# The modulation of the second block: from TensorE to ScalarE and GpSimd, and two half buffers beside the recurrence

## What is computed

```python
c_act = jax.nn.silu(c)                       # 1 x 1024
for l in range(2):
    mod = c_act @ w_ada[l] + b_ada[l]        # w_ada[l]: 1024 x 6144, mod: 1 x 6144
    sh_m, sc_m, gt_m, sh_f, sc_f, gt_f = jnp.split(mod, 6, axis=-1)
    h = rms_norm(x, g_mix[l]) * (1.0 + sc_m[:, None]) + sh_m[:, None]
    ...

def rwkv7_branch(u, ...):                    # first block
    for d, reverse in enumerate((False, True)):
        ...
        wkv = wkv + wkv7_scan(rh, heads(decay), kd, vh, -kk, kk * ah, reverse)
```

## Time and profile before

| | |
|---|---|
| median of the runs | 3211.61 us |
| profiled execution | 3216.43 us |
| its span | 3214.3 us, mean granted TensorE clock 0.940 |
| busy: TensorE | 2807.8 us (87%) |
| busy: VectorE | 1462.0 us (45%) |
| busy: ScalarE | 877.2 us (27%) |
| busy: GpSimd | 120.4 us (4%) |
| recurrence stage | about 122 to 790 us |

### The profile page before, as it was taken

How to read it: one execution, slowest core, us unless ns; L and a number is a source line. 1 busy time by engine, 2 the same in 40 slices (tenths; PEclk the granted TensorE clock), 3 DMA queues, 4 the chain that set the end, 5 groups by cost and what they waited for, 6 DMA issues and landing times.

```text
span 3214.3 us, 48264 instructions
## 1 busy us (share of the span) xinstructions
PE 2807.8 (87%) x21116; PEld 2057.9 (64%) x21116; DVE 1462.0 (45%) x2707; ACT 877.2 (27%) x1416; POOL 120.4 (4%) x199
## 2 busy tenths in 40 slices
PE   6898989868896877875798899999998888999999
PEld 5686767646573332321676667888876666778887
DVE  5545444467453110102565646434455665554433
ACT  3312212132430000001233353322223334433221
POOL 0010101010000000000000000000000000000000
PEclk9999999978997998997899999999999999999999
DMA  4353534332128999997233332333332342323332
GB/s 145 115 173 100 166 100 149 97 124 107 47 91 354 428 427 428 427 428 289 68 86 102 70 118 86 92 98 94 97 84 82 91 87 86 105 80 97 99 98 79
DMA packets 151816, 489.57 MB, mean 152 GB/s; under 512 B 13232, under 2 KB 41488, under 8 KB 139184
## 3 DMA queue, kind: packets, MB, share of 16 engines
q1 hardware_dynamic: 112256, 362.37, 31.5%
q0 software_dynamic: 26384, 97.32, 9.2%
q10 hardware_dynamic: 12960, 26.74, 2.6%
HBM read 456.49 MB, written 29.90 MB: 151 GB/s over the span
## 4 chain that ended last, share of the span: by engine, by line
PE 67%; DVE 14%; DMA 12%; ACT 5%; issue 2%; SPq 0%; POOL 0%; DVEq 0%; ACTq 0%; POOLq 0%
PE psum L154 64%; DMA wslot<-in_w_up 4%; DMA wslot<-in_w_gate 3%; DMA wslot<-in_w_down 3%; PE psum L157 3%; DVE halfL L163 2%; DVE sc__235 L193 1%; ACT halfH L160 1%; DVE m L190 1%; DVE slot L163 1%; DVE a20S L178 1%; DVE a21S L178 1%; ACT a1S L160 1%; DVE US L163 1%; DMA ada<-in_w_ada 0%
## 5 line engine op out<-in xcount | busy, mean ns | idle before, releaser
L163 DVE TENSOR_TENSOR halfL<-ring,halfH 128x1024 fp32r<-128x1024 f32 x302 | 367.5, 1221 | 684.6 <-ACT halfH L160 684.5
L160 ACT ACTIVATE halfH<-ring 128x1024 fp32r<-128x1024 f32 x302 | 316.5, 1053 | 808.4 <-PE psum L154 808.2
L154 PE MATMUL psum<-hH,halfH 128*128 128x512 f32 x1200 | 486.3, 405 | 9.7 <-DVE halfL L163 9.6
L154 PE MATMUL psum<-hL,halfH 128*128 128x512 f32 x1200 | 473.4, 394 | 0.0
L154 PE MATMUL psum<-hH,halfL 128*128 128x512 f32 x1200 | 472.3, 394 | 0.0
L154 PE MATMUL psum<-wslot,XT 128*64 128x512 f32 x1024 | 258.8, 664 | 73.7 <-DMA wslot<-in_w_gate 42.7
L154 PEld LDWEIGHTS psum<-hH,halfH 128*128 128x128 f32 x1200 | 228.5, 190 | 83.9 <-issue 23.4
L154 PEld LDWEIGHTS psum<-hH,halfL 128*128 128x128 f32 x1200 | 228.5, 190 | 49.6
L154 PEld LDWEIGHTS psum<-hL,halfH 128*128 128x128 f32 x1200 | 229.1, 191 | 44.6
L154 PEld LDWEIGHTS psum<-wslot,XT 128*64 128x64 f32 x1024 | 90.3, 152 | 241.3 <-issue 235.5
L154 PE MATMUL psum<-halfH,hH 128*128 128x512 f32 (+2 forms) x576 | 219.8, 382 | 11.8 <-DVE halfL L163 8.4
(11 more groups left out here) (446 smaller groups left out, 3909.9 us busy)
## 6 DMA issues: line engine op xcount, KB each, us to landing
wslot<-in_w_gate SPq DMA_DIRECT2D x32, 2048.0 KB, 30.0
...
ring<-in_w_in SPq DMA_DIRECT2D x120, 512.0 KB, 3.8
ada<-in_w_ada POOLq DMA_DIRECT2D x96, 512.0 KB, 4.2
ring<-in_w_gu SPq DMA_DIRECT2D x88, 512.0 KB, 3.6
ring<-in_w_down SPq DMA_DIRECT2D x44, 512.0 KB, 3.8
...
```

What stands on the lines that cost most here:

```text
L154: return self.e.matmul(*a, **k)
L160: return self.e.activation(*a, **k)
L163: return self.e.tensor_tensor(*a, **k)
```

## The change

1. TensorE no longer multiplies w_ada with cact. ScalarE scales each tile (now 128 x 512, 192 of them) in place by the column of `cact`, one scale per partition (`rw_scaled`). GpSimd adds the eight scaled tiles of a group into `ada_acc` (a copy and seven adds, two accumulators). TensorE sums the finished columns over the partitions: four matmuls per group of 512 columns, with `ada_acc` as the stationary operand and a column of ones, which gives columns at once; VectorE copies them to `mods`. `arow` and its turn are gone. There are 24 groups.
2. The order has two kinds of step now: `scaled`, 33 tiles in 20 preparation steps, and `ada`, at least three steps behind the last tile of its group. The last tile is scaled in step 22 of the fourth pass, and the last group is taken by TensorE in step 27.
3. The tiles are loaded on GpSimd's queue into six buffers: two where they were, four in the room of the third half buffer. The load of tile n + 6 waits for the sum of tile n. The loads begin when the last tile before the woven ones is used, so later than before.
4. The woven tiles use two half buffers instead of three (`half_of`, `half_before`), and are split one tile ahead instead of two. All other tiles use three, as before.
5. The loads of Zq and Zk and of the two gain rows move from GpSimd's queue to SyncE's, behind the last woven load.

```diff
--- before.py
+++ after.py
@@ -271,7 +271,6 @@
     cs, sn, t_pf, t_ang, t_k = (small("cs", 4, 8), small("sn", 4, 8), small("t_pf", 4), small("t_ang", 4, 8),
                                 small("t_k", 4, 8))
     t_pi = small("t_pi", 4, dt=I32)
-    arow = small("arow", 256)
 
     g8 = small("g8", 5)
     X = sb("X", AT_X, 4, 1024)
@@ -323,7 +322,7 @@
 
     WOVEN = [(tag, ci, ch) for tag, chs in (("q", G_q), ("k", G_k), ("v", G_v), ("g", G_gate))
              for ci, ch in enumerate(chs)]
-    LAST_WOVEN = len(tiles) - 1
+    FIRST_WOVEN, LAST_WOVEN = G_q[0].tiles[0][0], len(tiles) - 1
 
     def merge_chunks(branches, wo):
 
@@ -360,6 +359,13 @@
         G_ffn.append(part)
 
     LAST = len(tiles) - 1
+
+
+
+    half_of, half_before = [], []
+    for n in range(len(tiles)):
+        half_of.append(n % 2 if FIRST_WOVEN <= n <= LAST_WOVEN else n % NH)
+        half_before.append(max([m for m in range(n) if half_of[m] == half_of[n]], default=None))
 
 
     rk = Area(AT_FREE)
@@ -379,7 +385,8 @@
     st = [rk(f"st{d}", 2, 64) for d in range(2)]
     sp_ = [rk(f"sp{d}", 64) for d in range(2)]
     SA = [rk(f"SA{d}", 64) for d in range(2)]
-    ada_in = [rk(f"ada{i}", 1024) for i in range(2)]
+    ada_acc = [rk(f"ada_acc{i}", 512) for i in range(2)]
+    ada_in = [rk(f"ada{i}", 512) for i in range(2)] + [sb(f"ada{2 + i}", AT_HALF + 4096 + 512 * i, 512) for i in range(4)]
     stage = [rk(f"stage{i}", 512) for i in range(2)]
     spare = [rk(f"slot{i}", 512) for i in range(14)] + [sb(f"slot{14 + i}", AT_X + 512 * i, 512) for i in range(8)]
     kk, kds = spare[20], spare[21]
@@ -587,7 +594,7 @@
                                   ("rope", 0), ("rope", 1)] + [("turn", j) for j in range(6)])]
 
     def recurrence_order():
-        n_ada, woven, heads = 0, woven_steps(), list(A1_HEADS)
+        n_ada, n_scaled, woven, heads = 0, 0, woven_steps(), list(A1_HEADS)
         for pr in range(4):
             yield "head", pr
             for _ in range(2):
@@ -599,8 +606,12 @@
                         yield from next(woven, [])
                 if i in (1, 3) and pr:
                     yield ("gated", "turned")[i // 2], pr - 1
-                if n_ada < 108:
-                    yield "ada", n_ada // 9, n_ada % 9
+
+                while n_scaled < 192 and 20 * n_scaled < 33 * (N_PREP * pr + i + 1):
+                    yield "scaled", n_scaled
+                    n_scaled += 1
+                if n_ada < 24 and 33 * (N_PREP * pr + i - 3) >= 20 * (8 * n_ada + 8):
+                    yield "ada", n_ada
                     n_ada += 1
                 if pr == 3 and i > 1 and heads:
                     yield heads.pop(0)
@@ -615,7 +626,7 @@
                     yield from x
             if pr < 3:
                 yield "normed", pr
-        assert not heads
+        assert not heads and n_ada == 24
 
 
     BETWEEN = {**{1 + i: ("norming", 3, i) for i in range(9)}, 12: ("gated", 3), 14: ("turned", 3)}
@@ -719,7 +730,7 @@
 
         def gemm_bank(tag, ci, ch, ti, j, banks, stay, pair, ready=None):
             n, k0, nk = ch.tiles[ti]
-            H, L = tile_view(halfH[n % NH], n), tile_view(halfL[n % NH], n)
+            H, L = tile_view(halfH[half_of[n]], n), tile_view(halfL[half_of[n]], n)
             n_out = ch.w // 128 if stay == "weights" else 4
             pe.wait_ge(*at("lsplit", n))
             o = bank(banks[j]) if stay == "weights" else bank(banks[j])[:, 0:ch.w]
@@ -904,26 +915,15 @@
             turned(bank(b), US[:, pr, :]).then_inc(*up("rw_pe", "y_turned", pr))
             free[b] = [("yL", pr)]
 
-        def rw_ada(g, k):
+        def rw_ada(g):
+
             b = bank(ADA_BANK)
-            if k < 8:
-                n = 8 * g + k
-                if k == 0:
-                    pe.wait_ge(*at("cact"))
-                    clear(ADA_BANK)
-                pe.wait_ge(*at("ada_in", n))
-                for j in range(4):
-                    i = pe.matmul(b[32 * j:32 * j + 1, 0:256], cact[:, k:k + 1], ada_in[n % 2][:, j * 256:j * 256 + 256],
-                                  start=k == 0, stop=k == 7)
-                i.then_inc(*up("ada_pe", "ada", n))
-                return
-            pe.wait_ge(*at("ada_row", g))
-            if g:
-                pe.wait_ge(*at("mods", g - 1))
-            for c in range(2):
-                i = pe.matmul(b[:, 256 + 4 * c:260 + 4 * c], arow[:, c * 128:(c + 1) * 128], ident[:, 0:128:32],
-                              start=True, stop=True)
-            i.then_inc(*up("ada_pe", "ada_turned", g))
+            clear(ADA_BANK)
+            pe.wait_ge(*at("ada_sum", 8 * g + 7))
+            for c in range(4):
+                i = pe.matmul(b[:, c:c + 1], ada_acc[g % 2][:, c * 128:(c + 1) * 128], K("ones", 0, 1), start=True,
+                              stop=True)
+            i.then_inc(*up("ada_pe", "ada", g))
             free[ADA_BANK] = [("mods", g)]
 
 
@@ -1221,9 +1221,9 @@
             while done[0] <= min(n, last):
                 m = done[0]
                 ac.wait_ge(*at("tile_in", m))
-                if m >= NH:
-                    ac.wait_ge(*at("tile", m - NH))
-                ac.activation(tile_view(halfH[m % NH], m), tile_view(ring[m % NW], m),
+                if half_before[m] is not None:
+                    ac.wait_ge(*at("tile", half_before[m]))
+                ac.activation(tile_view(halfH[half_of[m]], m), tile_view(ring[m % NW], m),
                               COPY).then_inc(*up("split_act", "hsplit", m))
                 done[0] += 1
 
@@ -1292,7 +1292,7 @@
 
         def rw_gemm(n, ti, j):
             if j == 0:
-                split_to(WOVEN[n][2].tiles[ti][0] + 2, LAST_WOVEN)
+                split_to(WOVEN[n][2].tiles[ti][0] + 1, LAST_WOVEN)
 
         def rw_spill(n, j):
 
@@ -1323,12 +1323,12 @@
         def a1_turn(who, j):
             turned_out("a1", who, j, GEMM_BANKS[j % 4], *((qT, g8[:, 0:1]) if who == "q" else (kT, col("gqk", 1))))
 
-        def rw_ada(g, k):
-            if k == 7:
-                ac.wait_ge(*at("ada", 8 * g + 7))
-                for j in range(4):
-                    i = ac.activation(arow[32 * j:32 * j + 1, :], bank(ADA_BANK)[32 * j:32 * j + 1, 0:256], COPY)
-                    i.then_inc(*up("ada_act", *(("ada_row", g) if j == 3 else ())))
+        def rw_scaled(n):
+
+            ac.wait_ge(*at("cact"))
+            ac.wait_ge(*at("ada_in", n))
+            ac.activation(ada_in[n % 6], ada_in[n % 6], COPY,
+                          scale=cact[:, n % 8:n % 8 + 1]).then_inc(*up("ada_act", "scaled", n))
 
 
         sq_free = [None, None]
@@ -1539,7 +1539,7 @@
         ac.activation(US[0:64, 12, :], US[0:64, 12, :], ACT.Tanh).then_inc(*up("rw_act"))
         ac.activation(US[:, 13, :], US[:, 13, :], SIG).then_inc(*up("rw_act", "x_ready"))
         ac.wait_ge(*at("us", 11))
-        handlers = {"head": rw_head, "prep": rw_prep, "normed": rw_normed, "turned": rw_turned, "ada": rw_ada,
+        handlers = {"head": rw_head, "prep": rw_prep, "normed": rw_normed, "turned": rw_turned, "scaled": rw_scaled,
                     "gemm": rw_gemm, "spill": rw_spill, "square": a1_square, "root": a1_root, "turn": a1_turn,
                     "norming": rw_norming}
         for step, *args in recurrence_order():
@@ -1574,8 +1574,8 @@
             while done[0] <= min(n, last):
                 m = done[0]
                 ve.wait_ge(*at("hsplit", m))
-                ve.tensor_tensor(tile_view(halfL[m % NH], m), tile_view(ring[m % NW], m),
-                                 tile_view(halfH[m % NH], m).bitcast(F32), SU).then_inc(*up("split_dve", "lsplit", m))
+                ve.tensor_tensor(tile_view(halfL[half_of[m]], m), tile_view(ring[m % NW], m),
+                                 tile_view(halfH[half_of[m]], m).bitcast(F32), SU).then_inc(*up("split_dve", "lsplit", m))
                 done[0] += 1
 
         def ahead(ch, last=LAST_WOVEN):
@@ -1833,12 +1833,9 @@
         def a1_turn(who, j):
             turned_out("a1", who, j, GEMM_BANKS[j % 4], *((qT, g8[:, 0:1]) if who == "q" else (kT, col("gqk", 1))))
 
-        def rw_ada(g, k):
-            if k == 8:
-                ve.wait_ge(*at("ada_turned", g))
-                m = mods[:, 8 * g:8 * g + 8].rearrange("p (n c) -> p c n", c=2)
-                ve.tensor_copy(m, bank(ADA_BANK)[:, 256:264].rearrange("p (c n) -> p c n",
-                                                                       n=4)).then_inc(*up("ada_dve", "mods", g))
+        def rw_ada(g):
+            ve.wait_ge(*at("ada", g))
+            ve.tensor_copy(mods[:, 4 * g:4 * g + 4], bank(ADA_BANK)[:, 0:4]).then_inc(*up("ada_dve", "mods", g))
 
 
         H_ = "hd_dve"
@@ -2167,7 +2164,7 @@
 
         def modulated(L):
             D = "side_dve"
-            for g in range(12):
+            for g in range(24):
                 ve.wait_ge(*at("mods", g))
             if L:
                 ve.wait_ge(*at("f0", "x", 1, 1, 3))
@@ -2300,7 +2297,6 @@
 
 
         ve.wait_ge(*at("consts"))
```

(53 more changed lines are left out.)

## The result

The changed kernel takes 3239.64 us (median of four runs, 3236.64 to 3243.52) against 3212.19 in the same comparison, a ratio of 1.0087 (95% interval 1.0070 to 1.0104): slower by 27 us, where 24 us less were forecast. The profiled execution took 3236.64 us (span 3234.8), 20.2 more than that of before.

The account below looks back on a forecast made before the run. TensorE bounds the bodies, VectorE's chain the starts and much of the fourth pass; -26.6 - 2.3 - 12.5 - 4 + 3 + 1.1 + 5 + 12 = -24.3 us, median 3187.3. Likeliest case 3157 to 3219 (+7); range to 3243.

Parts of the forecast that it names:

- Bodies, -26.6: Steps 5 to 30 of the first three passes: TensorE loses the modulation's products, saving 26.6 us (17.6 to 34.1).
- Z stall, -12.5: Start of the fourth pass: Zq and Zk loaded from SyncE's queue end ScalarE's and VectorE's wait for Zq, -12.5 us.
- GpSimd's pace: Recurrence: GpSimd keeps up at 94% use in bodies; +5 us (0 to 12) put on the fourth pass for blocking.
- P: GpSimd's time per modulation tile (addition 1.23, issue 0.53, gap 0.28): 2.04 us, between 1.5 and 4.2.
- Rival (a): Bodies and fourth pass: GpSimd sets the pace; with 2.0 us additions net +31 us, 3243; chance 0.22.
- Contention, +12: Three starting chains and fourth pass: GpSimd's additions hold up VectorE's operations on two SBUF operands, +12 us (0 to 33).
- rival (b): Starting chains and fourth pass: the VectorE/GpSimd lock at full price, 33 us instead of 12, giving 3208; chance 0.12.
- ScalarE, +1.1: Step 0 of the first pass: two scalings stand ahead of the exponential that starts VectorE's chain, +1.1 us (0 to 2).
- rival (c): Bodies: the ada step was filler under an eviction's latency, so they gain half, -11 us, 3201; chance 0.06.
- The halves, "hidden": Recurrence: two half buffers, split one tile ahead, cost nothing; up to 2.4 us a tile if the cover is gone.
- The gate steps (-2.3): Starts of passes 1 and 2 and the fourth: ada steps ahead of VectorE's chain go, 0.64 + 0.64 + 1.0, -2.3 us.
- pass 4's idle and its new turns (-4 and +3): Fourth pass: six buffers and no ada step cut VectorE's idle, -4 (0 to -7.75); new turns on TensorE, +3 (2 to 5.6).

## Why the prediction failed

- **Bodies, -26.6:** right. -23.7 in the profile, -27.4 without the additions' 3.7. Steps of 3.60 us were said, and came.
- **Z stall, -12.5:** right, -12.4 by itself, and -12.6 in the changed kernel with short additions. With whole ones more than half of it is hidden, since the additions put 8 us back into the same start.
- **GpSimd's pace:** right in substance. P was taken as 2.04 and is 2.15, the addition 1.27 to 1.32 instead of 1.23; the term left out is 0.30 us for its own completion. Rival (a) needed 2.61 and did not come; no wait of TensorE on the sum in pass 4 shows, so its +5 was not spent. The sign that ScalarE would never wait for a tile in a body failed: 22.3 us, without a cost that shows. That the measured 3239.64 lies next to this rival's 3243, and so inside the stated range, is luck.
- **Contention, +12:** this step failed, and it decided the sign. The length of the additions costs 53 us by stages, 35.4 of them in the starts and 14.2 in pass 4's later steps, above even the upper end of 33. Three errors add up. I took a third of the bound because a DMA issue on top of TENSOR_TENSORs cost nothing; an issue is no addition, and the row says nothing of one. I counted 6 additions in three chains; the order puts 8 or 9 into each of four starts. And I priced 17 additions in pass 4 where 30 lie in its later steps alone, on a chain that VectorE carries all through. The mechanism of rival (b), which I gave 0.12, is what happened, and even its full price was too small.
- **ScalarE, +1.1, and rival (c):** neither shows clearly. Short scalings gain nothing once the additions are short, though the start of pass 0 stays 2.4 us long with short additions; a body step lost the full 0.54 us.
- **The halves, "hidden":** right in the passes, wrong at their edge. I compared the waits tile by tile within the recurrence, where n + 1 - 2 equals n + 2 - 3, and not for the first two tiles, which are split in the loop before it, where no lead was given up: +5.4 us.
- **The rest of the program:** I held it fixed. The router gave +5.1, some 3 of it with the clock.
- **Sum:** by its own steps, with what the runs show: -23.7 bodies, -12.4 Z, +53.3 less the 3.7 already in the bodies, +5.4, +5.1, -3.0 to the rows' store make +21.0; +20.2 was profiled. The gate steps (-2.3) don't show: the starts without additions, 69.9 and 69.5, are as long as before. Of pass 4's idle and its new turns (-4 and +3) -2.1 came, 73.5 without additions against 75.6. The +7 (3219) was also added up wrong: it keeps the -4 of pass 4's idle, whose high end is 0, and without it is +11 (3223), still below what was measured.

The page SBUF — State Buffer of the Trainium skill, section Who interferes with whom, calls the shared port pair an exclusive lock for which a VectorE instruction with two SBUF inputs contends with a GpSimd one that reads SBUF. The runs agree as far as they go: 0.69 becomes 2.02 under back-to-back additions, and 0.686 stays with an operand in PSUM. TENSOR_SCALARs with one operand out of SBUF were held as well here, 1.052 instead of 0.542, which that sentence does not cover. I had cited it and then discounted it for a row that did not bear on it.
